# Squares folded on GpSimd, a reordered opening, and four modulation pieces on GpSimd

## The reference, cut to what matters

```python
def rmsnorm(x, g):
    y = xf * lax.rsqrt(jnp.mean(xf * xf, axis=-1, keepdims=True) + EPS)
    return (y * g.astype(jnp.float32)).astype(x.dtype)
...
cond = jax.nn.silu(c)
for i in range(DEPTH_2):
    mod = cond @ w_ada[i] + b_ada[i]
    sh1, sc1, g1, sh2, sc2, g2 = jnp.split(mod, 6, axis=-1)
    h = rms_norm(x, ln_mix_g[i]) * (1.0 + sc1[:, None, :]) + sh1[:, None, :]
    ...
    x = x + g1[:, None, :] * y
    h = rms_norm(x, ln_mlp_g[i]) * (1.0 + sc2[:, None, :]) + sh2[:, None, :]
    x = x + g2[:, None, :] * (jnp.square(jax.nn.relu(h @ w_mlp_in[i])) @ w_mlp_out[i])
```

## Time and profile before

| | us |
|---|---|
| median of 3 runs (lowest, highest) | 1314.45 (1313.77, 1316.89) |
| profiled execution, and its span | 1315.27, 1313.5 |
| TensorE busy | 1290.3 |
| VectorE, ScalarE, GpSimd busy | 950.7, 657.9, 88.5 |
| one w_hi, one w_lo (128x2048) | 1.905, 2.286 |
| one panel's 48 products on TensorE | 5.7 |

### The profile page before, as it was taken

The page is one execution under the profiler, slowest core; times in us unless marked ns, Lnnn a source line. Parts: engine busy times, 40 slices in busy tenths (PEclk is TensorE's granted clock), DMA queues, the critical chain, the costliest instruction groups (busy, mean ns, idle before and its releaser), DMA issues.

```text
span 1313.5 us, 24511 instructions
## 1 busy us (share of the span) xinstructions
PE 1290.3 (98%) x10581; PEld 1237.9 (94%) x10581; DVE 950.7 (72%) x1199; ACT 657.9 (50%) x872; POOL 88.5 (7%) x134
## 2 busy tenths in 40 slices
PE   7999999999999999999999999999999999999998
PEld 7999999999999999999989689999999888999998
DVE  5769897764797667777776978877789666754443
ACT  4544436364643434343657747454456455654441
POOL 4003000000000000020100000100000020000000
PEclk9999999999999999999999999999999999999999
DMA  9665555545488777885632046999875431465550
GB/s 280 202 206 176 182 176 166 187 135 179 161 288 297 258 258 267 284 284 166 209 128 92 6 161 225 322 313 325 312 235 168 165 97 65 161 192 193 180 174 33
DMA packets 172701, 259.67 MB, mean 198 GB/s; under 512 B 5157, under 2 KB 147794, under 8 KB 172594
## 3 DMA queue, kind: packets, MB, share of 16 engines
q1 hardware_dynamic: 160906, 203.13, 47.1%
q0 software_dynamic: 10848, 53.69, 11.6%
q10 hardware_dynamic: 840, 1.28, 0.3%
HBM read 257.03 MB, written 1.05 MB: 196 GB/s over the span
## 4 chain that ended last, share of the span: by engine, by line
PE 86%; DVE 8%; ACT 3%; issue 2%; DMA 1%; SPq 0%; POOL 0%; ACTq 0%; DVEq 0%
PE ring L675 59%; PE acc L675 24%; ACT w_hi L1503 2%; DVE w_lo L2051 2%; PE acc L1276 1%; DVE arena L2100 1%; PE ring L1085 1%; DMA raw<-in_w_in_dram 1%; ACT h_hi L1503 1%; ACT arena L1503 1%; DMA arena<-in_w_ada_dram 1%; DVE arena L2464 0%; DVE h_lo L2096 0%; DVE h_lo L2094 0%; DVE norm L2066 0%
## 5 line engine op out<-in xcount | busy, mean ns | idle before, releaser
L675 PE MATMUL ring<-h_hi,w_hi 128*128 128x256 f32 (+1 forms) x2016 | 575.0, 285 | 5.7 <-DVE w_lo L2051 1.8
L675 PE MATMUL ring<-h_hi,w_lo 128*128 128x256 f32 (+1 forms) x2016 | 568.2, 282 | 0.0
L675 PE MATMUL ring<-h_lo,w_hi 128*128 128x256 f32 (+1 forms) x2016 | 566.5, 281 | 0.0
L2051 DVE TENSOR_TENSOR w_lo<-raw,w_hi 128x2048 fp32r<-128x2048 f32 x189 | 430.9, 2286 | 165.4 <-ACT w_hi L1503 164.7
L1503 ACT ACTIVATE w_hi<-raw 128x2048 fp32r<-128x2048 f32 x191 | 363.2, 1905 | 132.1 <-PE ring L675 64.0
L675 PEld LDWEIGHTS ring<-h_hi,w_hi 128*128 128x128 f32 x2016 | 379.8, 188 | 11.8 <-issue 7.3
L675 PEld LDWEIGHTS ring<-h_lo,w_hi 128*128 128x128 f32 x2016 | 380.7, 189 | 2.6 <-issue 2.2
L675 PEld LDWEIGHTS ring<-h_hi,w_lo 128*128 128x128 f32 x2016 | 380.9, 189 | 0.0
L675 PE MATMUL acc<-e_hi,w_hi 128*128 128x256 f32 x768 | 216.9, 282 | 2.9 <-DVE e_lo L2752 1.5
L675 PE MATMUL acc<-e_hi,w_lo 128*128 128x256 f32 x768 | 215.1, 280 | 0.0
L675 PE MATMUL acc<-e_lo,w_hi 128*128 128x256 f32 x768 | 215.1, 280 | 0.0
(11 more groups left out here) (317 smaller groups left out, 1348.2 us busy)
## 6 DMA issues: line engine op xcount, KB each, us to landing
arena<-in_w_ada_dram POOLq DMA_DIRECT2D x64, 768.0 KB, 6.3
raw<-in_w_mlp_in_dram SPq DMA_DIRECT2D x32, 1024.0 KB, 5.8
raw<-in_w_mlp_out_dram SPq DMA_DIRECT2D x32, 1024.0 KB, 5.0
raw<-in_w_in_dram SPq DMA_DIRECT2D x24, 1024.0 KB, 5.8
raw<-in_w_e_gate_dram SPq DMA_DIRECT2D x16, 1024.0 KB, 6.3
raw<-in_w_e_up_dram SPq DMA_DIRECT2D x16, 1024.0 KB, 5.4
raw<-in_w_e_down_dram SPq DMA_DIRECT2D x16, 1024.0 KB, 5.0
raw<-in_diff_w_in_dram SPq DMA_DIRECT2D x12, 1024.0 KB, 5.3
```

Source lines behind the costliest of these rows:

```text
L675: return nc.tensor.matmul(dst, lhs, rhs, start=start, stop=stop, **kw)
L2051: tt(w_lo[q % RAW][:, 0:n], raw[q % RAW][:, 0:n], w_hi[q % SPL][:, 0:n].bitcast(F32), ALU.subtract)\
```

## The change

**Folding.** For the norms x, ffn and m1 GpSimd adds the squares of blocks 0 to 3 into one block (`fold`), and TensorE sums that one and blocks 4 and 5 behind the last panel (`stat_front`), and 6 and 7 as before: five products of ones for eight.

**Opening.** The gain of the mix norm is loaded by a DMA of its own and transposed by itself; the first two blocks are scaled ahead of the first w_lo; the second panel is split in two halves, each with parts of its own (`two_halves`); the third panel is loaded ahead of the memory; the memory's norm is made by rows (squares with row sums on ScalarE, root, reciprocal, scaling on VectorE) before its transposes, which stand behind the panel a_val0; its gain is applied when the transposes are taken from PSUM.

**Modulation.** GpSimd makes layer 1's pieces 0 to 3 itself (`ada_piece`): a scaling for the first, a scaling and a sum for each of the others. VectorE's piece 4 stands behind residual step 2 of n_o. A few semaphores are shared between stages, with no wait more or less.

The diff, cut to its core:

```diff
@@ -597,6 +600,14 @@
+            sq = blk(SQX, 8)
+            def fold(tag):
+                pool.wait_ge(*sig(tag + "_squared", 2))
+                nc.gpsimd.tensor_tensor(sq[:, 0:2], sq[:, 0:2], sq[:, 2:4], ALU.add).then_inc(S(tag + "_folded"), 1)
+                pool.wait_ge(*sig(tag + "_folded", 1))
+                nc.gpsimd.tensor_tensor(sq[:, 0], sq[:, 0], sq[:, 1], ALU.add).then_inc(S(tag + "_folded"), 1)
...
@@ -604,6 +615,18 @@
+            def ada_piece(n):
+                pool.wait_ge(S(f"ada_landed{n % 2}"), 16 * (16 + n // 2 + 1))
+                pool.wait_ge(S("ada_used"), 32 + n)
+                piece, so_far = flat(ADA_RAW, (n % 2) * ADA_W, ADA_W), flat(ADA, 0, ADA_W)
+                if n == 0:
+                    nc.gpsimd.tensor_scalar(so_far, piece, cond[:, 0:1], None, ALU.mult).then_inc(S("ada_used"), 1)
+                else:
+                    nc.gpsimd.tensor_scalar(piece, piece, cond[:, n:n + 1], None, ALU.mult).then_inc(S("ada_scaled"), 1)
+                    pool.wait_ge(S("ada_scaled"), n)
+                    nc.gpsimd.tensor_tensor(so_far, so_far, piece, ALU.add).then_inc(S("ada_used"), 1)
...
@@ -615,6 +638,12 @@
                 for n in range(ADA_FIRST):
                     ada_load(turn, l, n, at(n))
+                    if l == 0 and n == 1:
+                        fold("ffn")
+                    if l == 1 and n:
+                        ada_piece(n - 1)
+                if l == 1:
+                    ada_piece(ADA_FIRST - 1)
...
@@ -625,6 +654,7 @@
+            fold("x")
             pool.wait_ge(*sig("xo_ready", 4))
...
@@ -829,6 +860,23 @@
+            def two_halves(p, f):
+                open_fill(f)
+                wh = w_hi[p % SPL][:].rearrange("p (k n) -> p k n", k=KB)
+                wl = w_lo[p % RAW][:].rearrange("p (k n) -> p k n", k=KB)
+                for b in range(2):
+                    if b == 0:
+                        pe.wait_ge(S("first_half_split"), 1)
+                    else:
+                        open_panel(p)
+                    o, c = bank(f)[:, b * T:(b + 1) * T], slice(b * P, (b + 1) * P)
+                    for k in range(KB):
+                        mm(o, wh[:, k, c], h_hi[:, k, :], k == 0, False)
+                        mm(o, wh[:, k, c], h_lo[:, k, :], False, False)
+                        last = mm(o, wl[:, k, c], h_hi[:, k, :], False, k == KB - 1)
+                last.then_inc(S("panel_done"), 1)
...
@@ -855,6 +903,16 @@
+            def stat_front(tag):
+                f, sq = FL[tag + "_stat"], blk(SQX, 8)
+                open_fill(f)
+                pe.wait_ge(*sig(tag + "_folded", 2))
+                mm(bank(f)[:, 0:T], ones[:], sq[:, 0], True, False)
+                pe.wait_ge(*sig(tag + "_squared", 3))
+                for k in (4, 5):
+                    mm(bank(f)[:, 0:T], ones[:], sq[:, k], False, False)
...
@@ -881,22 +939,28 @@
             turn_rows(lambda i: bank(FL["x_t"] + i), 0, "x_turned")
+            pe.wait_ge(S("mix_gain_landed"), 16)
+            open_fill(FL["mix_gain"])
+            nc.tensor.transpose(bank(FL["mix_gain"])[:, 0:KB], vec_in[0:KB, 0, :], ident[0:KB, 0:KB]).then_inc(S("mix_gain_turned"), 1)
...
-            keep_busy(FL["a_gate"], 5)
+            keep_busy(FL["a_gate"], 4)
...
-                mm(acc[0][:, t * P:(t + 1) * P], ones[:], blk(MEM_T)[:, 0, t * P:(t + 1) * P], True, True)
-            pe.wait_ge(S("vecs_landed"), 16 * N_VEC_DMA)
+                last = mm(acc[0][:, t * P:(t + 1) * P], ones[:], blk(MEM_T)[:, 0, t * P:(t + 1) * P], True, True)
+            last.then_inc(S("mix_spread"), 1)
+            keep_busy(FL["a_gate"], 2)
+            pe.wait_ge(S("vecs_landed"), 16 * (N_VEC_DMA - 1))
...
-            keep_busy(FL["a_gate"], 8)
-            full("a_gate", split="mix_ready", together=1)
-            pe.wait_ge(S("mem_landed"), 16)
+            keep_busy(FL["a_gate"], 4)
+            linear_first([PN["a_gate"]], FL["a_gate"], block_ready("mix_ready"))
+            two_halves(PN["a_gate"] + 1, FL["a_gate"] + 1)
+            linear(PN["a_val"], FL["a_val"], KB, 2, lambda k: h_hi[:, k, :], lambda k: h_lo[:, k, :])
+            pe.wait_ge(S("mem_rows"), 2)
             turn_rows(lambda i: acc[i], 2048, "mem_turned")
-            full("a_val")
-            stats("mem", lambda k: blk(SQ + k)[:, 0], "mem_squared")
+            linear(PN["a_val"] + 1, FL["a_val"] + 1, KB, 2, lambda k: h_hi[:, k, :], lambda k: h_lo[:, k, :])
...
@@ -936,7 +1000,7 @@
                     linear_last("x", PN["w_o"] + i, FL["w_o"] + i)
-                stat_pair("x", i - 1)
+            stat_front("x")
...
@@ -1006,9 +1070,8 @@
-                stat_pair("ffn", i - 1)
...
-            stat_pair("ffn", 2)
+            stat_front("ffn")
...
             raw_first("ffn", PN["moe"], half_bank(moe_fill(0)), {3: (3,)})
...
@@ -1473,15 +1536,13 @@
-            stat_pair("m1", 0)
             linear_last("m1", PN["d_o"] + 3, FL["d_o"] + 3)
-            stat_pair("m1", 1)
-            stat_pair("m1", 2)
+            stat_front("m1")
...
@@ -1589,7 +1650,8 @@
-            vec_loads(act, VEC_SOURCES(a)[:9])
+            vec_loads(act, VEC_SOURCES(a)[:1], "mix_gain_landed")
+            vec_loads(act, VEC_SOURCES(a)[1:9])
...
@@ -1600,16 +1662,27 @@
-            ahead(2 - SPL)
+            act.wait_ge(S("raw_landed1"), 16)
+            for b, sem in ((0, "first_half_hi"), (1, "hi_made")):
+                c = slice(b * P, (b + 1) * P)
+                func(w_hi[1][:].rearrange("p (k n) -> p k n", k=KB)[:, :, c], raw[1][:].rearrange("p (k n) -> p k n", k=KB)[:, :, c],
+                     ACT.Copy).then_inc(S(sem), 1)
+            made["hi"] += 1
+            ahead(3 - SPL)
+            act.wait_ge(S("mix_ready"), KB)
+            act.wait_ge(S("mem_landed"), 16)
+            for t in range(2):
+                last = func(blk(SQ + 4 * t, 4), arena[:, 2048 + t * D:2048 + (t + 1) * D].rearrange("p (b t) -> p b t", b=4),
+                            ACT.Square, accum_out=stat[:, 4 + t:5 + t])
+            last.then_inc(S("mem_squared"), 1)
+            act.wait_ge(S("mem_squared"), 1)
+            func(stat[:, 6:8], stat[:, 4:6], ACT.Sqrt, scale=1.0 / D, bias=eps[:]).then_inc(S("mem_squared"), 1)
             ahead(0)
...
-            act.wait_ge(S("mix_ready"), KB)
-            squares_of("mem", blk(MEM_T, 8), blk(SQ, 8), lambda j: act.wait_ge(S("early_steps"), 3 + j))
...
-            root("mem")
...
@@ -2072,16 +2145,7 @@
-            def scaled(tag, src, dst, gain, nb=KB):
-                inverse(tag)
-                chain.settle()
-                for b in range(nb):
-                    last = stt(dst(b), src(b), gain(b), norm[:, 2, :], ALU.mult, ALU.mult)
-                    if b % 2:
-                        last.then_inc(S(tag + "_scaled"), 1)
-            def split_norm(tag, gain, shift=None, mid=SQX, row=None):
+            def split_norm(tag, gain, shift=None, mid=SQX, row=None, behind_two=None):
...
@@ -2100,6 +2164,8 @@
+                        if behind_two is not None:
+                            behind_two()
                         low(0)
...
@@ -2163,19 +2229,36 @@
-            ahead(1 - SPL)
+            dve.wait_ge(S("mix_gain_turned"), 1)
+            drains(nc.vector.tensor_copy(mix_gain[:], bank(FL["mix_gain"])[:, 0:KB]), FL["mix_gain"])
+            dve.wait_ge(S("mix_spread"), 1)
+            chain.did(nc.vector.tensor_copy(norm[:, 2, :], acc[0][:, 0:T]))
+            drained_wait(dve, FL["x_t"] + 3)
+            drained_wait(dve, FL["mix_gain"])
+            split_norm("mix", lambda b: mix_gain[:, b:b + 1], mid=SQ, row=2, behind_two=lambda: ahead(1 - SPL))
+            for b, sem, split in ((0, "first_half_hi", "first_half_split"), (1, "hi_made", "panel_split")):
+                c = slice(b * P, (b + 1) * P)
+                dve.wait_ge(S(sem), b + 1)
+                tt(w_lo[1][:].rearrange("p (k n) -> p k n", k=KB)[:, :, c], raw[1][:].rearrange("p (k n) -> p k n", k=KB)[:, :, c],
+                   w_hi[1][:].bitcast(F32).rearrange("p (k n) -> p k n", k=KB)[:, :, c], ALU.subtract).then_inc(S(split), 1)
+            made["lo"] += 1
...
-            chain.did(nc.vector.tensor_copy(norm[:, 2, :], acc[0][:, 0:T]))
-            drained_wait(dve, FL["x_t"] + 3)
-            split_norm("mix", lambda b: vcol("mix_g", b), mid=SQ, row=2)
+            ahead(3 - SPL)
+            dve.wait_ge(S("mem_squared"), 2)
+            chain.did(nc.vector.reciprocal(stat[:, 6:8], stat[:, 6:8]))
+            chain.settle()
+            for t in range(2):
+                rows = arena[:, 2048 + t * D:2048 + (t + 1) * D]
+                ts(rows, rows, stat[:, 6 + t:7 + t], None, ALU.mult).then_inc(S("mem_rows"), 1)
             ahead(0)
...
                 dve.wait_ge(S("mem_turned"), i + 1)
-                nc.vector.tensor_copy(blk(MEM_T, 8)[:, 2 * i:2 * i + 2].rearrange("p b t -> p (b t)"), acc[i][:])\
-                    .then_inc(S("early_steps"), 1)
+                for b in range(2):
```

(10 more changed lines are left out.)

40 lines of the change are left out of this document (22 added, 18 removed).

## The result

The changed kernel takes **1330.9 us** (median of 4, 1328.8 to 1331.2) against 1315.3 (median of 4); the ratio is 1.0113 with a 95% interval of 1.0097 to 1.0129. It is 1.1% slower: the direction of the forecast, nearly four times its size, and outside its range. (The median of 1314.45 at the start was of three runs of the kernel before; a fourth moved it to 1315.3.) The profiled execution took 1328.78, its span is 1326.9, so 13.4 us over the span before.

The account below looks back on a forecast made before the run. TensorE was taken as the bound, busy for 1290.3 of 1313.5 us. The terms summed as 1315.27 - 6.6 - 1.9 + 14.0 - 1.5 = 1319.3, or 1318.5 us in terms of the median; the range was 1309 to 1325.

Parts of the forecast that it names:

- The opening: Start of the kernel up to the memory's norm: TensorE gains 6.6 us, between 3.3 and 6.6.
- All three terms: At the start: first product 1.5 us earlier, second panel's 1.8 us gap gone, memory's ones products gone for 3.3 us.
- The first one: First real product at 16.6 instead of 18.09, 1.5 us earlier, as the norm copy no longer waits for the vectors.
- The folding: Norms x, ffn and m1: three ones products fewer each, gaining 1.9 us in sum, between 0 and 3.7.
- the reason given: Norm m1: its last pair starts right behind ScalarE's squares, which end last there, so nothing is gained.
- The stage of n_o: Ahead of the first MLP: piece 4 waits for load 4 behind GpSimd's pieces; TensorE starts at 807.4, 14.0 us lost.
- the price of a scaling on GpSimd: GpSimd's pieces ahead of the first MLP: 2.2 us chosen per scaling, between 1.01 (VectorE's own) and 7.7.
- Given back: Second chunk of the first MLP: piece 4 no longer stands ahead of e_lo, so TensorE's wait goes, 1.5 us.
- "milder form" of the long pieces: Modulation pieces: VectorE and GpSimd block each other, loss grows by 4.6 us, time 1323.1; long or blocked pieces together 0.14.

## Why the prediction was wrong

*The opening*: forecast 6.6 us, measured 7.7. All three terms came. The first one was 2.4 instead of 1.5: w_hi of the first panel also started 1.0 us earlier (10.31 for 11.29), since its panel landed earlier, which the prediction didn't expect.

*The folding*: forecast 0.7, 1.2 and 0 for x, ffn and m1; measured 0.5, 1.1 and 0. Right, and m1 for the reason given.

*The stage of n_o*: the mechanism was right (piece 4 ahead of the low parts waits for load 4, which waits for piece 3), and so was what hung on it. The step that failed is the price of a scaling on GpSimd, which only bounds of 1.0 and 7.7 were known for: "I choose 2.2, nearer the low end". It took 4.16 to 4.37, four times in the chain. Measured from h_lo at the start of the stage to TensorE's first product, the forecast was 35.8 us (807.4 - 771.6) and the trace has 43.6 (805.74 - 762.10), 7.8 more. By terms: scalings 8.1 more (4.16 + 4.37 + 4.17 + 4.16 against 4 x 2.2); sums 1.3 more, all in the one beside VectorE's w_lo at 776.49 (4.84; the others took 3.42, for 3.45 forecast); gaps between GpSimd's instructions 1.7 more (2.3, for issues and semaphores, where the forecast had only 0.6 of waiting for load 2); load 0 landed 1.6 earlier than forecast and load 4 1.6 (4.7 for 6.3). That is 8.1 + 1.3 + 1.7 - 3.2 = 7.9. The range failed by the same step: 7.7 instead of 2.2 for each of four scalings is 22 us, and the upper end of 1325 lay only 6.5 above the forecast.

*Left out*: what follows the wait, 2.0 us from the first product to the root. The run with TensorE kept at work gives 1.1 of it to the clock; the rest is the last residual and its squares in VectorE's and ScalarE's queue, of which the prediction said that they need no more than TensorE's own steps.

*Given back*: forecast 1.5, measured 1.0.

Sum of the trace: -7.7 - 0.5 - 1.1 - 0.2 (not assigned) + 21.9 + 2.0 - 1.0 = +13.4, the difference of the spans. The lag by the medians is 15.6; GpSimd's idle time ahead of its first load, most of which is the sparse attention, was 134.4 to 139.0 us in the profiles, though the kernels are the same there, so single profiles differ by some us for a reason that stays open.

*The rivals*: the "milder form" of the long pieces was in the profile: GpSimd's sum was held for 1.4 us by w_lo and a scaling for 0.2. It cost little in the changed kernel, because VectorE stood idle most of the time. With piece 4 back at its old place GpSimd's pieces cost 7.5 us, through held operations and the clock behind TensorE's waits. I had priced it at 4.6 and seen only one side of it, VectorE stopping GpSimd; the other, GpSimd stopping the low parts that TensorE waits for, is what counted.

## What to carry to other kernels

Work moved to an engine with room on average must be followed in its own row to the first result that somebody waits for; here that took a chain of seven operations, and the transfer behind it, onto the path. When the trace doesn't show an operation and four of them stand in a chain, carry both of its bounds through the chain into the range; here they lay 22 us apart, more than the whole forecast loss. Count a wait of TensorE with the slower clock that can follow it: 3.0 us of waiting cost another 1.7 here. And look for idle time just ahead of a wait for another engine: piece 4 fitted into 1.91 us ahead of the reciprocal, and was free there.

## What the runs showed of the hardware

GpSimd scaled 128x1536 fp32 by a scalar per partition in 4.16 us, slower than its product of the same size with a broadcast column (2.75) and than its sum of two full inputs (3.41).

A VectorE operation with two inputs in SBUF waits for a GpSimd operation that is under way, a scaling as well as a sum (3.52 us for 0.48, 1.52 for 0.17, 3.84 and 5.03 for 2.29). The other way round, a GpSimd sum beside VectorE's w_lo took 4.84 for 3.41, and a product 4.15 for 2.75. VectorE went on 0.1 to 0.2 us before the recorded end of a sum and 1.0 to 1.1 before that of a scaling.

TensorE's granted clock was 0.50 after a wait of 21.5 us, and stayed full with idle products in it; behind that wait, where other engines came last, this was worth 1.1 us. It also fell to 0.50, with TensorE at work again, behind waits of 2.06, 2.96 and 3.02 us, at a cost of an estimated 1.7 us each time. It stayed full behind the wait of 1.52 us in the kernel with VectorE's pieces.
